# Expert units of 32 rows in four column quarters, in place of 64 rows in two halves

## The reference

```
def moe_ffn(h, router_w, router_b, w_gate_up, b_gate_up, w_down, b_down):
    ...
    logits = (xt @ router_w + router_b).astype(jnp.float32)
    top_v, top_i = lax.top_k(logits, TOP_K)
    gates = jax.nn.softmax(top_v, axis=-1)
    ...
    counts = jnp.bincount(e_flat, length=N_EXPERTS)
    ...
```

## Time and profile before

| | us |
|---|---|
| median of 3 runs | 1927.23 |
| lowest, highest | 1924.39, 1931.75 |
| the profiled execution, its time | 1936.22 |
| the profiled execution, its span | 1934.7 |

### The profile page before, as it was taken

The page is one execution under the profiler, slowest core; times in us unless marked ns, Lnnn a source line. Parts: engine busy times, 40 slices in busy tenths (PEclk is TensorE's granted clock), DMA queues, the critical chain, the costliest instruction groups (busy, mean ns, idle before and its releaser), DMA issues. The chain is left out here.

```text
span 1934.7 us, 41919 instructions
## 1 busy us (share of the span) xinstructions
PE 1799.1 (93%) x14459; PEld 1113.3 (58%) x14459; DVE 1024.7 (53%) x1632; ACT 795.5 (41%) x1163; POOL 240.8 (12%) x302
## 2 busy tenths in 40 slices
PE   5999889589999999999999799999999759998897
PEld 2999754555555555555555355555555436777853
DVE  3785443654555554554454345545455473884665
ACT  3334532244444444444444344444444443433511
POOL 0000000011111111111111011111111120350000
PEclk8999999689999999999999899999999979999999
DMA  7773572249967998799499998999999662221001
GB/s 278 252 249 120 157 204 111 92 171 369 422 257 300 410 427 313 293 421 394 143 404 427 427 427 352 406 427 372 401 426 427 263 231 76 77 77 46 30 30 44
DMA packets 129677, 520.06 MB, mean 269 GB/s; under 512 B 13587, under 2 KB 52260, under 8 KB 80324
## 3 DMA queue, kind: packets, MB, share of 16 engines
q1 hardware_dynamic: 116722, 483.41, 63.9%
q0 software_dynamic: 12736, 35.17, 4.9%
q10 hardware_dynamic: 146, 0.48, 0.1%
HBM read 494.10 MB, written 24.90 MB: 268 GB/s over the span
## 5 line engine op out<-in xcount | busy, mean ns | idle before, releaser
L1878 DVE COPY ring<-staging 128x2048 f32 (+1 forms) x385 | 474.5, 1232 | 508.6 <-PE banks L1739 313.2
L1739 PE MATMUL banks<-ring,rowsT 128*64 128x256 f32 x6144 | 700.7, 381 | 3.4 <-ACT rowsT L1828 3.4
L1739 PEld LDWEIGHTS banks<-ring,rowsT 128*64 128x64 f32 x6144 | 443.3, 138 | 310.7 <-issue 78.5
L1810 ACT ACTIVATE ring<-staging 128x2048 f32 (+1 forms) x193 | 369.0, 1912 | 339.5 <-PE banks L1739 277.5
L1765 PE MATMUL banks<-ring,hiddenT 128*64 128x512 f32 x1536 | 375.4, 610 | 0.5 <-PEq L1796 0.3
L1765 PEld LDWEIGHTS banks<-ring,hiddenT 128*64 128x64 f32 x1536 | 93.8, 137 | 137.2 <-issue 113.0
L1816 ACT ACTIVATE glu<-banks 128x128 f32<-128x128 f32 x192 | 53.2, 277 | 281.1 <-DVE lin L1884 281.1
L586 PE MATMUL banks<-w_in_hi,hT 128*128 128x256 f32 (+1 forms) x768 | 147.8, 292 | 1.0 <-issue 1.0
L2212 PE MATMUL banks<-h3T,w_in_hi 128*128 128x512 f32 x400 | 130.4, 408 | 1.4 <-DVE h3T L2388 1.4
L586 PEld LDWEIGHTS banks<-w_in_hi,hT 128*128 128x128 f32 x768 | 122.9, 194 | 3.0 <-issue 3.0
L1692 POOL DMA_DIRECT2D expert_rows<-y_rows x94 | 52.5, 559 | 527.3 <-ACT y_rows L1834 526.4
(11 more groups left out here) (408 smaller groups left out, 1790.6 us busy)
## 6 DMA issues: line engine op xcount, KB each, us to landing
staging<-in_w_gate_up SPq DMA_DIRECT2D x250, 1024.0 KB, 12.5
staging<-in_w_down SPq DMA_DIRECT2D x128, 1024.0 KB, 12.5
stage<-in_w_mod SPq DMA_DIRECT2D x24, 1024.0 KB, 5.4
stage<-in_w_in SPq DMA_DIRECT2D x25, 512.0 KB, 4.0
expert_rows<-y_rows POOLq DMA_DIRECT2D x94, 128.0 KB, 5.9
stage<-in_w_in SPq DMA_DIRECT2D x11, 1024.0 KB, 6.1
expert_rows<-catT SPq DMA_DIRECT2D x1, 7936.0 KB
early<-in_w_gate_up SPq DMA_DIRECT2D x6, 1024.0 KB, 11.7
```

What stands on the lines that cost most here:

```text
L1739: mm = pe.matmul(k.bank(j % 2)[c * SLOTS:(c + 1) * SLOTS, 0:UP], rowsT[:, kk, half, :], w[:, kk * WIDE + c * UP:kk * WIDE + (c + 1) * UP], ...
L1810: act.activation(ring[:, pos % RING, :], staged(e, c), ACT.Copy).then_inc(act_filled, 1)
L1878: dve.tensor_copy(ring[:, pos % RING, :], staged(e, c)).then_inc(dve_filled, 1)
```

## The change

`SLOTS` becomes 32. A row is now gathered and stored as four quarters of 256 numbers, so `rows` and `y_rows` are 128x256. `up` takes a stationary operand of 32 rows (128x32) and 128 moving columns, four products side by side, at partitions 0, 32, 64 and 96; `down` likewise with 256 columns. A unit has `STEPS` = 2 steps, each with two calls of `up` (two chunks each) and two chunks of `down`, of the step before (two before, so far). The chunks' places in the ring (`POSITION`) change with it. The bias has its high and low parts in two tiles and takes two products a step.

`picked` is gone: the router's stage puts each unit's expert into a bank by one product, and VectorE compares it once into a table `picks`, of which `pick` takes a column per unit. The plan has packed words, from which ScalarE and VectorE read the experts before, of and after a unit with one load. GpSimd gathers three units ahead of the loop, then in each turn gathers unit i+2 before it stores, with one DMA a unit. The write of zeros takes 32 partitions (62 x 32 rows). The router's `at_code` and `slots` get 512 columns, and its two product operands are fp32r.

```diff
-SLOTS = 64
+SLOTS = 32
+PARTS = P // SLOTS
...
-        at_code = sb("at_code", [P, 2, TOPK, CODES])
+        at_code = sb("at_code", [P, 2, TOPK, CODES], F32R)
...
-PAIRS = 4
+STEPS = 2
 WIDE = 2 * UP
-POSITION = (0, 1, 3, 4, 6, 7, 8, 9, 10, 11, 14, 17)
+POSITION = (0, 1, 2, 3, 6, 7, 8, 9, 10, 11, 16, 17)
...
-                gather(0)
-                load_picked(0)
-                load_picked(1)
-                gather(1)
-                with pool.Fori(1, units) as i:
-                    load_picked(i + 1)
-                    gather(i + 1)
-                    store_rows(i)
+                gather(0)
+                gather(1)
+                gather(2)
+                with pool.Fori(1, last) as i:
+                    gather(i + 2)
+                    store_rows(i)
+                store_rows(last)
...
+                    for low in range(2):
+                        mm = pe.matmul(k.bank(s)[:, 0:UP], pick[:], bias[:, low, s * UP:(s + 1) * UP],
+                                       start=(low == 0), stop=False, skip_group_check=True)
...
+                        for kk in range(KT // 2):
+                            for c in range(PARTS):
+                                mm = pe.matmul(k.bank(s)[of_part(c), two * P:(two + 1) * P],
+                                               rowsT[:, kk % 2, 2 * half + kk // 2, :],
+                                               w[:, kk * WIDE + c * P:kk * WIDE + (c + 1) * P],
...
+                    for s in range(STEPS):
+                        g = STEPS * i + s
+                        up(i, s, 0)
+                        turn_hidden(g - 1, 1 - s)
+                        if s == 0:
+                            add_bias(i, 1)
+                        else:
+                            turn_rows(i + 1)
+                            add_bias(i + 1, 0)
+                        up(i, s, 1)
+                        down(g - 1, i, 1 - s)
...
-                dve.wait_ge(bias_in, 64)
-                lins = raw_bias[:].rearrange("p (j two n) -> p j two n", two=2, n=P)[:, :, 1, :]
+                chain(dve.tensor_scalar(picks[:], k.bank(7)[:, 0:P], k.eps[:, 2:3], None, ALU.is_equal))
+                dve.wait_ge(bias_in, 32)
+                lins = raw_bias[:].rearrange("p (j two n) -> p j two n", two=2, n=CH)[:, :, 1, :]
```

More of the change, by code:

```diff
@@ L16 @@
 I32 = mybir.dt.int32
+I16 = mybir.dt.int16
 U32 = mybir.dt.uint32
@@ L40 @@
 ENDS = 2 * P
-TABLE = ENDS + NE + LINE
+AROUND = ENDS + NE
+TABLE = AROUND + P + LINE
 UP = 2 * P
@@ L138, in token_constant, with blocks_constant @@
     token = np.arange(S, dtype=np.float32).reshape(NT, P).T
[L139 to L147, removed]
+    part, inside = np.arange(P) // SLOTS, np.arange(P) % SLOTS
+    return np.ascontiguousarray(np.concatenate([token, part[:, None], inside[:, None]], 1).astype(np.float32))
+def blocks_constant():
+    i = np.arange(P) // SLOTS
+    return np.ascontiguousarray((i[:, None] == i[None, :]).astype(np.float32))
 def pool_constant():
@@ L1646, in loads @@
                         arrived(first, m - AHEAD)
[L1648 to L1652, removed]
+                sp.dma_start(raw_bias[:], d["b_gate_up"]).then_inc(bias_in, 16)
+                sp.dma_start(blocks, d["blocks"]).then_inc(bias_in, 16)
                 for m in range(EARLY - AHEAD):
@@ L1661, in _ @@
                 sp.wait_ge(y_read, last + 1)
-                for part in range(2):
-                    sp.dma_start(rows_of(part, last * SLOTS), y[part * SLOTS:(part + 1) * SLOTS, :]).then_inc(last_out, 16)
-                sp.wait_ge(last_out, 32)
+                sp.dma_start(rows_of(last * SLOTS), y_parts).then_inc(last_out, 16)
+                sp.wait_ge(last_out, 16)
             @block.gpsimd
             def _(pool):
-                units = units_on(pool)
-                by_half = d["h2"].rearrange("t (h n) -> (t h) n", h=2)
+                last = last_on(pool)
+                by_part = d["h2"].rearrange("t (h n) -> (t h) n", h=PARTS)
                 def code(i):
@@ L1748, in turn_hidden, with down @@
                         after(pe, hT_ready, g - 1)
-                        pe.transpose(k.bank(2 + j % 2)[:, 0:P], hidden[:, j % 2, :], ident).then_inc(turned_ps, 1)
-                def down(g, i, j):
-                    step = (j + 2) % PAIRS
+                        pe.transpose(k.bank(2 + s)[:, 0:P], hidden[:, s].rearrange("p a n -> p (a n)"), ident
+                                     ).then_inc(turned_ps, 1)
+                def down(g, i, s):
+                    first = 6 * (1 - s) + 4
@@ L1926, in _ @@
                 dve.wait_ge(bias_high, 1)
-                for part in range(2):
-                    low = slice((2 * part + 1) * NE, (2 * part + 2) * NE)
-                    ins = dve.tensor_tensor(bias[low, :], raw_bias[low, :], f(bias[low, :]), ALU.subtract)
-                ins.then_inc(bias_ready, 1)
+                dve.tensor_tensor(bias[:, 1, :], raw_bias[:], f(bias[:, 0, :]), ALU.subtract).then_inc(bias_ready, 1)
+                fill(0, 0, 2)
+                fill(0, 0, 3)
                 steps(0, None, 0, expert_on(dve, 1))
                 with dve.Fori(1, units) as i:
-                    steps(i, expert_on(dve, i - 1), expert_on(dve, i), expert_on(dve, i + 1))
-                last = last_on(dve)
-                end = PAIRS * last
-                linear(end + 3, 3, last * CHUNKS + 11)
-                finish_hidden(end + 3, 3)
-                dve.wait_ge(dve_filled, units * len(BY_DVE) + 2)
-                dve.sem_inc(dve_filled, 1)
+                    steps(i, *around(dve, i))
+                dve.wait_ge(dve_filled, units * len(BY_DVE) + 3)
                 fill(units, NE - 1, 5)
```

298 lines of the change are left out of this document (151 added, 147 removed).

## The result

The changed kernel takes 1949.32 us in the median of 4 runs (1945.15 to 1950.98), the kernel before 1927.51 of 4 (1924.39 to 1931.75): ratio 1.0108, 95% interval 1.0083 to 1.0133. The change costs 1.1%, 22 us by these medians (the later runs of the kernel before had medians of 1929.2 to 1930.0, against which it is 19 to 20). I had forecast 1938 (1912 to 1978), with a chance of 0.54 for slower. The measured cost is twice the forecast one of 11 us. The profiled execution took 1945.15 us, span 1943.5.

What follows compares the result with a forecast made beforehand. TensorE and the DMA feed of weights were taken as two close limits, the feed binding short experts after the change. Stage +13, start -6.8, end -0.8, clock +4.5 make +10: 1946 us profiled, median 1938, range 1912 to 1978.

Steps and rivals of the forecast that it cites:

- The sum: Whole kernel: expert stage, start, end and lower clock together +10 us, for a median of 1938 us.
- the clock: Expert stage: more stalls put TensorE's granted clock at its lower level, +4.5 us, from 0 to 15.
- The feed (the main step): Expert stage: each expert costs the larger of its computation and its weight loading; stage 1157 against 1144.1, +13 us.
- The unit: Expert stage: one unit of 32 rows takes 12.4 us, from 12.1 to 12.8, against 23.24 for 64 rows.
- the credit of 28: Expert stage: chunks loaded ahead under long experts save about 4 us at each of 7 runs of short experts.
- the remainder of 4: Expert stage: 4 us added to the experts' summed costs, taken as the same as in the kernel before.
- The start: Before the expert stage: no `picked` transfer, first ups earlier, larger router tables take back 1.8 us; together -6.8 us.
- The end: End of the expert stage: one store issue in place of two, -0.8 us.
- The zeros: Write of zeros to `expert_rows` from 32 partitions instead of 64: costed at nothing.
- The rival with half the rate: Write of zeros at half rate from 32 partitions, so the stage waits: +35 us, 1973 us; chance 0.06.
- Groups of four: Rival in TensorE's products: weight loads of four side by side don't overlap, unit of 13.4 us, 1969 to 1984; chance 0.13.
- GpSimd late: Rival: GpSimd's store or gather late by 1 us in each computing unit, +31 to 46, 1969 to 1984; chance 0.05.

Runs made afterwards that it cites:

- before_again: The kernel before, unchanged, profiled once more: 1929.24 us (10 runs), ratio 0.9998.
- after_half: The changed kernel with only half of each weight chunk of experts 4 to 31 loaded: 1798.81 us, ratio 0.9326 to the kernel before.
- act_waits: The changed kernel with ScalarE instead of GpSimd waiting for the store's landing, before it reads the next output: 1949.19 us.
- store_first: The changed kernel with GpSimd's store ahead of its gather in the loop: 2015.76 us, ratio 1.0451 to the kernel before.
- one_bias: The changed kernel without the second bias product of each step (the bias's low part left out): 1939.63 us, ratio 1.0049 to the kernel before.
- before_start: The kernel before with `picked` loaded ahead of the first gather and fp32r operands in the router's slot products: 1926.28 us (12 runs), again 1924.49 (10 runs).
- before_picked: The kernel before with the load of `picked` ahead of the first gather: 1926.95 us (12 runs), ratio 0.9988.
- one_unit: The changed kernel with every expert cut to one unit of 32 rows: 1733.69 us, one run.

## Why the prediction came out as it did

**The sum.** On the two profiles it was made for, it reads: forecast +10, measured 1945.15 - 1936.22 = +8.9. That is close by luck. The stage cost 21.6 us where I had 17.5 with the clock, and all outside it gave 12.7 where I had 7.6. By the medians the change costs 22 us, twice what I wrote, and only the width of the range holds it. The difference between the two readings is in the base: the profiled execution of before lay 9 us above its median, that of after 4 below its own. Against before_again the spans are 15.4 us apart. A sum on one profiled pair carries some 7 us of such chance, nearly as much as the forecast itself.

**The feed (the main step).** Right for experts of one kind in a row: 1 and 2 units cost 30.1 and 30.7 us by the sum whatever TensorE does, 30.1 and 30.9 measured. That the feed is what TensorE waits for is shown by the halved feed, where I expected 1802 and 1903 and got 1799 and 1907. The stage became 21.6 us longer (24 against before_again) where +13 and +4.5 of clock were forecast.

Expert by expert the bound doesn't hold. By the row turns of the changed kernel 8 of its 14 experts of two units took under 29 us, which I had named as a sign of being wrong. All 20 short experts took 536.7 us where the sum has 610.4, and the 46 units of the longer ones 612.9, 13.3 each, where it has 570.4. Chunks loaded ahead make the first experts of a run short, and the wait for the run's last chunks falls into the first units of the long expert behind it. Only a run and its long experts together come out as summed. Two more signs were missed for the same reason: the DMA engines moved 357 GB/s in the mean and not 427 over most of the stage, and VectorE's waits for SP's chunks grew to 167.6 us (251.7 with ScalarE's), not to several hundred.

**The unit.** Forecast 12.4 us from a range of 12.1 to 12.8. A unit that waits for nothing takes 12.10: so do most units of after_half and five of the changed kernel, such as the one from 577.20 to 589.30. So the fours cost nothing, and the bias 0.23 where I had 0.4. Nearly all other units of the changed kernel without a long wait take 12.46 to 12.65. The feed isn't what adds the 0.4: in the expert of 7 units, where the DMA engines move 48 GB/s (above), five units in a row take 12.46 to 12.49. What goes with it in the traces is where GpSimd's issue of the gather falls. Such a unit of the changed kernel, with its row turn at 903.86, and one of after_half with 12.11 us and its row turn at 871.60:

```profile
904.41 1.95 PE L1751 MATMUL banks<-ring,rowsT 128*32 128x128 f32 x64
905.15 1.30 POOL L1698 DMA_INDIRECT rows<-h_rows,slot  x1 [3.78 <-PE banks L1727]
906.07 1.43 DVE L1900 COPY ring<-staging 128x2048 f32 x1 [0.47 <-PE banks L1751]
906.50 1.99 PE L1784 MATMUL banks<-ring,hiddenT 128*32 128x256 f32 x32
```

```profile
871.14 3.64 DVE L1902 COPY ring<-staging 128x2048 f32 x3
872.15 1.95 PE L1753 MATMUL banks<-ring,rowsT 128*32 128x128 f32 x64
872.89 2.00 POOL L1700 DMA_INDIRECT rows<-h_rows,slot  x1 [3.28 <-PE banks L1729]
873.92 1.91 PE L1786 MATMUL banks<-ring,hiddenT 128*32 128x256 f32 x32
```

In the first, VectorE's copies have a gap in which the gather's issue ends early (1.30 us), the next copy starts 2.21 us behind the row turn and takes 1.43, and `down` starts 2.09 us behind its ups. In the second the three copies follow each other, the issue takes 2.00 us and ends behind them, and `down` starts after 1.77. Among units of at most 12.8 us, 33 of the changed kernel have such a copy that starts 2.2 us or more behind the row turn, and all 33 take 12.46 to 12.65; act_waits has 46, all of 12.47 to 12.70. after_half, store_first and one_bias have none, and their units go down to 12.10, 12.10 and 11.87. That the two engines get in each other's way is suggested by this and not shown: no run moved the gather's issue alone. The 33 units at 0.37 us are 12 us, an estimate of the most that it costs. It may be little: one_bias has no such unit, and gained 9.7 us in all, which the bias products alone would explain.

By the sum's own terms, with measured sizes: 6 x 30.1 + 14 x 30.9 + 46 x 12.55 = 1190.5, less the credit of 28 and with the remainder of 4, is 1166.5 for a measured 1165.7. The terms that were too small are the unit, 0.15 us in 46 units (+7), and the two-unit expert, 0.2 us in 14 (+3). With them the separate +4.5 for the clock isn't needed; what the lower clock cost wasn't measured by itself.

**The credit and the remainder.** The total of 28 fits, and not for my reason. With the sizes above, the row turns of the changed kernel give each of the first six runs, with the long experts behind it, a credit of 1.6 to 3.4 us, 16 together, where I had 24. The last run (experts 29 to 31), with nothing behind it, took 66.1 us for 90.3, 24 less, while the end of the stage costs 16 where I had a remainder of 4. The remainder stood in the sum without its working: 28.6 - 19.0 leaves 9.6. Over the whole stage before, the row turns show 24.3 us above 23.24 a unit, which leaves 4.3. An experiment without the four chunks ahead wasn't run.

**The start.** Forecast -6.8, measured -10.6 (-8.8 against before_again). The part on `picked` and the gather as what is late next was right. The step that failed is "+1 to +3, I take 1.8" for the router's larger tables: fp32r operands more than paid for them. A product of 512 columns in fp32r is one record where one of 256 columns in 32 bits was two. In the router's timeline the last products before the plan's end were 6.29 us for eight products (16 records), and are 2.07 for four (the kernel before, then the changed one). In the first ups this edit alone is worth 4.65 us by before_start against before_picked and 1.9 by before_start_2, the second profile of that kernel; the medians of before_picked and before_start differ by 0.7. I had seen the type in the diff and priced only the width.

```profile
366.34 6.29 PE L1307 MATMUL banks<-at_code,at_slot 128*128 128x256 f32 x16
...
364.56 2.07 PE L1311 MATMUL banks<-at_code,at_slot 128*128 128x512 f32 x4 [1.53 <-DVE at_code L1455]
```

**The end.** Forecast -0.8, measured +0.25 (from the last products to the next stage's first, 5.70 and 5.95 us). One store issue less didn't show.

**The zeros.** Right: nothing. The rival with half the rate is out (46.6 us of wait, not 84). The write is 8.1 MB, where I had 7.9. By the Trainium skill, "SBUF - State Buffer", Door 1, 32 and 64 partitions reach the same ports; the trace agrees, with waits of 46.6 us from 32 partitions and 46.2 from 64.

**Groups of four.** The rival is out: 1.77 us for 64 records, 0.1106 us for each four where half of a pair's 0.2225 would be 0.111. (A step of the kernel before has two chunks of 8 products, so 32 records, not of 16 products as I wrote ahead of the prediction.) The Trainium skill ("TensorE: Matmul & The Clock Gate", Part 3) says that weight loads overlap only where the row group differs. By its 2.38x for three column tiles I had estimated a unit of nearly 15 us; the trace disagrees with 12.10 to 12.65, and the measurement decides.

**GpSimd late.** I gave it 0.05. A late store or gather didn't cost units: act_waits took ScalarE's waits for a free output tile from 32.2 to 11.2 us, and the time didn't move. store_first shows how near it is: one swap in GpSimd's queue costs 66 us. A cost of the gather's issue itself, as it may stand in the 0.4 us above, wasn't among my rivals. The store's landing grew from 5.9 us to 8.7 in the median.

## What to carry to other kernels

Halving the work per block helps only blocks that compute for longer than their weights take to arrive. Before a tuned loop is made finer, divide the bytes per expert by the rate that the profile shows at its best, and count the blocks that fall below: here 20 of 32, and a TensorE freed of 98 us gave nothing back. Then ask how far the buffers let a long block pay for the short ones behind it, and sum over a run of short blocks together with the long one, since single blocks can lie far from the bound on either side. Waits for a DMA's landing belong behind every issue that others need soon, since GpSimd's queue runs in order.

## What the runs showed of the hardware

- Two profiles of one kernel differed by 6.6 us, spread over all stages, and the medians of two versions whose expert stage ended 10.4 us apart differed by 3.7 to 4.8. Where the rest goes wasn't found.
- In one_unit, TensorE's granted clock was 0.75 of full speed in the mean of 880 us, and the experts still took the 30.1 us of their feed (29.8 to 30.5): a slow clock costs nothing under a transfer.

```profile
420.00:1300.00 880.00, 513.59 (x9528) 361.71 (x9528) 311.41 (x379) 256.75 (x290) 64.25 (x87) 0.75 1.01 427
```
